# The first gate rows of two expert passes: the first expert pair's tokens gathered in other parts and banks

## The reference, cut to what matters

```python
def moe_ffn(h, expert, gate, w_gate, w_up, w_down):
    ...
    xb = h[slot_tok].reshape(n_blocks, MOE_BLOCK, D)
    def expert_block(args):
        xblk, e = args
        return (jax.nn.silu(xblk @ w_gate[e]) * (xblk @ w_up[e])) @ w_down[e]
    yb = lax.map(expert_block, (xb, block_expert))
    y = yb.reshape(n_pad, D) * slot_gate[:, None].astype(h.dtype)
    return jnp.zeros_like(h).at[slot_tok].add(y)
```

## Time and profile before

| | us |
|---|---|
| median of three runs | 1698.57 (1698.17 to 1700.7) |
| the profiled execution's own time | 1696.97 |
| its span | 1695.2 |
| TensorE busy | 1647.9 (97%) |
| ScalarE busy | 288.5 (17%) |
| VectorE busy | 448.9 (26%) |
| mean transfer rate | 352 GB/s |

### The profile page before, as it was taken

One profiled execution on the slowest core, in us unless ns is written; L12 is line 12 of the kernel. 1 busy time (PEld: TensorE's weight loads), 2 busy tenths in 40 slices (PEclk: granted clock), 3 DMA queues, 4 the chain that ended last, 5 costly groups with the idle time before them and its releaser, 6 DMA issues.

```text
span 1695.2 us, 20421 instructions
## 1 busy us (share of the span) xinstructions
PE 1647.9 (97%) x8806; PEld 940.7 (55%) x8806; DVE 448.9 (26%) x940; ACT 288.5 (17%) x584; POOL 62.4 (4%) x92
## 2 busy tenths in 40 slices
PE   9999999999899999999999999899999999999997
PEld 7784433433333785634334333348787888866554
DVE  1470000000000325300000000025266657722222
ACT  2301101101010222111011000112222122321212
POOL 4000000000000100000000000005000000000000
PEclk9999999999999999999999999999999999999999
DMA  9889999999999956899999999999254445699996
GB/s 335 327 323 376 429 428 427 426 429 427 424 430 426 390 195 241 331 426 427 429 427 427 428 425 428 427 407 331 93 199 149 153 145 198 251 403 425 424 424 282
DMA packets 88203, 597.46 MB, mean 352 GB/s; under 512 B 6072, under 2 KB 17072, under 8 KB 53920
## 3 DMA queue, kind: packets, MB, share of 16 engines
q1 hardware_dynamic: 84480, 586.30, 85.4%
q0 software_dynamic: 3616, 9.65, 1.7%
HBM read 594.88 MB, written 1.05 MB: 352 GB/s over the span
## 4 chain that ended last, share of the span: by engine, by line
PE 59%; issue 26%; DMA 12%; DVE 2%; POOL 1%; ACT 0%; SPq 0%; POOLq 0%; DVEq 0%
PE psum L952 31%; DMA ring<-in_w_gate_dram 10%; PE psum L658 8%; PE psum L645 4%; PE psum L602 3%; PE psum L935 3%; PE psum L1046 2%; DMA ring<-in_w_up_dram 1%; PE psum L652 1%; PE psum L893 1%; PE psum L1085 1%; PE psum L1062 1%; POOL rstd L3339 1%; PE psum L780 1%; PE psum L808 0%
## 5 line engine op out<-in xcount | busy, mean ns | idle before, releaser
L952 PE MATMUL psum<-ring,xT 128*64 128x512 f32 (+1 forms) x2024 | 417.2, 560 | 29.4 <-DMA ring<-in_w_up_dram 10.5
L952 PEld LDWEIGHTS psum<-ring,xT 128*64 128x64 f32 x2024 | 144.9, 137 | 273.4 <-issue 244.7
L952 PE MATMUL psum<-ring,work 128*64 128x512 f32 x992 | 219.9, 593 | 0.1
L2615 DVE TENSOR_TENSOR work<-work,psum 128x512 f32<-128x512 f32 (+1 forms) x45 | 40.9, 910 | 573.0 <-PE psum L952 567.6
L952 PEld LDWEIGHTS psum<-ring,work 128*64 128x64 f32 x992 | 70.8, 137 | 135.5 <-issue 131.6
L645 PE MATMUL psum<-xT,ring 128*128 128x256 f32 x512 | 113.6, 380 | 0.0
L1925 ACT COPY work<-psum 128x512 f32<-128x512 f32 (+1 forms) x45 | 23.2, 515 | 489.9 <-PE psum L1062 489.9
L658 PE MATMUL psum<-ring,mkv 128*128 128x256 f32 x456 | 104.9, 380 | 0.0
L645 PEld LDWEIGHTS psum<-xT,ring 128*128 128x128 f32 x512 | 96.3, 190 | 13.8 <-issue 0.8
L658 PE MATMUL psum<-ring,xT 128*128 128x256 f32 x400 | 92.0, 379 | 0.3 <-issue 0.3
L658 PEld LDWEIGHTS psum<-ring,mkv 128*128 128x128 f32 x456 | 85.7, 190 | 11.8 <-DVE work L3188 0.3
(11 more groups left out here) (378 smaller groups left out, 1646.8 us busy)
## 6 DMA issues: line engine op xcount, KB each, us to landing
ring<-in_w_down_dram SPq DMA_DIRECT2D x49, 2048.0 KB, 22.2
ring<-in_w_up_dram SPq DMA_DIRECT2D x49, 2048.0 KB, 21.8
ring<-in_w_gate_dram SPq DMA_DIRECT2D x48, 2048.0 KB, 20.3
ring<-in_w_in_dram SPq DMA_DIRECT2D x16, 2048.0 KB, 11.1
ring<-in_w_exp_up_dram SPq DMA_DIRECT2D x15, 2048.0 KB, 19.1
work<-in_w_gate_dram SPq DMA_DIRECT2D x10, 2048.0 KB, 13.1
ring<-in_w_exp_down_dram SPq DMA_DIRECT2D x10, 2048.0 KB, 20.7
work<-in_w_exp_gate_dram SPq DMA_DIRECT2D x9, 2048.0 KB, 15.6
```

Source lines behind the costliest of these rows:

```text
L952: ins = pe.matmul(to[part * CAP:(part + 1) * CAP, 0:n], lhsT=lhsT, rhs=w[:, half * n:(half + 1) * n], start=first, stop=last)
L2615: dve.tensor_tensor(by_rows(h[:, 0:F], j), in_order(silu[:, 0:F], j), in_order(u_bank[:, 0:F], j), ALU.mult).then_inc(sem("h"), 1)
```

## The change

Part 0 of the first group is gathered in two halves that are counted, copied and waited for apart: chunks 0 and 1 into `m_bank`, chunks 2 and 3 into `y_bank`. Gate chunks 0 and 1 wait for the first copy, gate chunks 2 and 3 for the second. Part 1 goes into `u_bank`: its chunks 4 and 5 are gathered behind gate chunks 0 and 1, its chunks 6 and 7 behind gate chunks 2 and 3. Gate chunks 4 to 7 wait for its copy. In passes with groups of two the semaphores `gathered` and `xe` count one more, so everything that waits on them is shifted by one (`gathers`).

```diff
-                                ... gathered=E, xe=E, ...
+                                ... gathered=E + (not pairs), xe=E + (not pairs), ...
...
+            def gathers(self, g, part):
+
+                return self.group * g + part + (self.group == 2)
...
-                def gather(g, part, to, first=0, end=None):
+                def gather(g, part, to, first=0, end=None, signals=True):
...
-                    if end is None:
+                    if signals:
                         ins.then_inc(sem("gathered"), 1)
...
-                        pe.wait_ge(sem("xe"), plus(ph.group * g + part, B["xe"]))
+                        pe.wait_ge(sem("xe"), plus(ph.gathers(g, part), B["xe"]))
                         gather(g, part, to)
...
                 elif first == 0:
-                    gather(0, 0, m_bank)
-                    gather(0, 1, y_bank, 0, 2)
+                    gather(0, 0, m_bank, 0, 2)
+                    gather(0, 0, y_bank, 2)
                     pe.wait_ge(sem("xe"), plus(1, B["xe"]))
                     up("gate", g_bank, 0, range(2))
-                    gather(0, 1, y_bank, 2)
+                    gather(0, 1, u_bank, 0, 2, False)
+                    pe.wait_ge(sem("xe"), plus(2, B["xe"]))
                     up("gate", g_bank, 0, range(2, 4))
-                    pe.wait_ge(sem("xe"), plus(2, B["xe"]))
+                    gather(0, 1, u_bank, 2)
+                    pe.wait_ge(sem("xe"), plus(3, B["xe"]))
                     up("gate", g_bank, 0, halves[1])
...
                 elif first == 0:
-                    tokens(0, 0, m_bank)
-                    tokens(0, 1, y_bank)
+                    for c, of in ((0, m_bank), (2, y_bank)):
+                        act.wait_ge(sem("gathered"), plus(c // 2 + 1, B["gathered"]))
+                        act.copy(ph.tokens(0, 0)[:, c:c + 2, :], of[:, c * P:(c + 2) * P].rearrange("p (c s) -> p c s", c=2)).then_inc(sem("xe"), 1)
+                    tokens(0, 1, u_bank)
                     gate(0)
...
-                        dve.wait_ge(sem("gathered"), plus(ph.group * g, B["gathered"]))
+                        dve.wait_ge(sem("gathered"), plus(ph.gathers(g, 0), B["gathered"]))
```

More of the change, by code:

```diff
@@ L393, in __init__ @@
                 self.per = dict(used=self.pieces, silu=E, h=E + 1, t_full=E + 1, hT=E + 1, last_part=1 + pairs, y=2 * E + 2 if pairs else E + 1, y_lo=2 * E + 2 if pairs else 0, slot_gate=E // 2 if pairs else 0,
-                                pick=TC * E // self.group, pickg=2 * E, gathered=E, xe=E, pick_turned=E // 2 if pairs else E, pickT=E // 2 if pairs else E, scattered=4, shift=1, piece=16 * self.pieces // RAW, tail=16 + self.ahead, half=2, early=32)
+                                pick=TC * E // self.group, pickg=2 * E, gathered=E + (not pairs), xe=E + (not pairs), pick_turned=E // 2 if pairs else E, pickT=E // 2 if pairs else E, scattered=4, shift=1, piece=16 * self.pieces // RAW, tail=16 + self.ahead, half=2, early=32)
                 times = MORE if more else 1
@@ L1154, in hand_out @@
                         pe.wait_ge(S("rows_in"), (32, 80)[phases.index(ph)])
-                        pe.wait_ge(sem("xe"), B["xe"] + N_EXP)
+                        pe.wait_ge(sem("xe"), B["xe"] + N_EXP + 1)
                     else:
@@ L1863, in tokens @@
                 def tokens(g, part, of):
-                    act.wait_ge(sem("gathered"), plus(ph.group * g + part + 1, B["gathered"]))
+                    act.wait_ge(sem("gathered"), plus(ph.gathers(g, part) + 1, B["gathered"]))
                     act.copy(ph.tokens(g, part), of.rearrange("p (c s) -> p c s", c=DC // ph.group)).then_inc(sem("xe"), 1)
```

## The result

The changed kernel takes 1700.86 us in the median (1699.65 to 1703.7, 20 runs), the kernel before 1698.46 us (1697.26 to 1700.7, 20 runs) on the same chip: +2.4 us, ratio 1.0016 with a 95% interval of 1.001 to 1.0022. It is slower, by a little less than the 3.4 us that I had called the bound of what can be told; with twenty runs each the difference is clear of zero. I had forecast -0.8 us. The profiled execution is 1700.63 us long, its span is the first row here; the page shows nothing else.

The account below looks back on a forecast made before the run. Weight transfers were taken to end both expert passes; an unbroken stream 0.4 us earlier in each, with TensorE's 1.16 us delay absorbed by its waits, summed to -0.8 us from 1698.57, giving 1697.8 us, range 1696.0 to 1701.2.

Parts of the forecast that it names:

- the stall: TensorE's new wait before gate chunk 4 for the copy of part 1, forecast at 0.75 us a pass.
- A2: Third early 1 MB weight transfer of a pass, issued at 137.60; forecast 1.16 us later, at 138.76.
- A0: First early 1 MB weight transfer of a pass, issued at 132.93; forecast 0.84 us earlier, at 132.09.
- A1: Second early 1 MB weight transfer of a pass, issued at 135.89; forecast 0.84 us earlier, at 135.05.
- the dry microsecond: Stretch 132.5 to 133.5 at a pass's start, transfers at only 33 GB/s; forecast to go.
- unbroken stream: Transfers running without gaps after a pass's start; forecast to begin 0.17 to 0.67 us earlier, taken as 0.4 us.
- A4: First 2 MB transfer after the four 1 MB ones, issued at 142.75; forecast issued at 143.91, flowing from 144.5.
- close, but not dry: Claim that A4, flowing from 144.5, arrives before A3 ends at 144.8, so the transfers never run empty there.
- A3: Fourth early 1 MB weight transfer of a pass, issued at 139.32; forecast issued at 140.48 and ending at 144.8.
- TensorE's delay through: Rival: TensorE's 1.16 us delay at chunk 4 reaches each pass's end, +2.3 us, 1700.9, if transfers don't end passes; chance 0.10.
- rows 3: Profile rows of TensorE's weight waits, the last just ahead of 544.99 and 1095.23, read as transfers ending each pass.
- dry twice more: Rival: A2 and A4 meet an empty queue, each losing 0.5 us; 0 to +0.6 us a pass, up to 1699.8; chance 0.18.

Follow-up runs that it names:

- e2: Changed kernel with part 1's chunks 6 and 7 gathered right behind chunks 4 and 5, ahead of gate chunks 2 and 3: 1698.62 us against 1698.53 for the kernel before.
- e3: Kernel before with only the gather of chunks 6 and 7 moved behind gate chunks 2 and 3: 1701.24 us against 1698.53.
- e5: Kernel before with four idle TensorE products ahead of expert 0's down rows in both passes: 1703.24 us against 1698.25.
- e6: Kernel before with four idle TensorE products ahead of expert 1's up rows in both passes: 1699.44 us against 1698.25.
- e7: Kernel before with four idle TensorE products ahead of expert 4's up rows in both passes: 1698.23 us against 1698.25.
- e10: Kernel before with four idle TensorE products ahead of expert 0's up rows in both passes: 1706.71 us against 1698.38.
- e4: Kernel before with four idle TensorE products ahead of gate chunk 4 in both passes: 1707.19 us against 1698.53.
- e1: Kernel before with all sixteen gather products in one run ahead of gate chunk 0: 1698.57 us against 1698.53.
- e13: Kernel before with six of the eight gather products of the first group's part 1 left out: 1697.62 us against 1698.43.

## Why the prediction was wrong

*TensorE's part was right.* Gate rows 0.90 us earlier (0.84 forecast), the stall 0.67 us (0.75), chunk 4 and A2 onward 1.09 us later (1.16); the copies, VectorE's marks and the silu moved without anyone waiting for them. A0 and A1 came 0.90 us earlier, and the dry microsecond went: 229 GB/s from 4 to 5 us behind the first gather instead of 139.

*The step that failed* is the one that follows the transfers: "From there TensorE frees 2 MB each 3.43 us and the transfers need 4.9. So the unbroken stream starts 0.17 to 0.67 us earlier". I had drawn the rate of the frees from two issues and stopped at A4. A4 (142.75) was the last issue that I weighed, as "close, but not dry", and between 146 and 160 us I had looked at no row of the transfers. The rows that I should have gone on to read, the later issues of the kernel before:

```profile
146.19 0.33 SPq L3468 DMA_DIRECT2D ring<-in_w_down_dram  x1
149.62 0.33 SPq L3468 DMA_DIRECT2D work<-in_w_up_dram  x1
155.80 0.33 SPq L3471 DMA_DIRECT2D work<-in_w_up_dram  x1
161.36 3.76 SPq L3471 DMA_DIRECT2D ring<-in_w_gate_dram  x2
```

and their sizes, with the last column the us from issue to landing (issues from 140 to 150 us):

```profile
work<-in_w_down_dram SPq DMA_DIRECT2D x1, 2048.0 KB, 9.3
ring<-in_w_down_dram SPq DMA_DIRECT2D x1, 1536.0 KB, 9.8
work<-in_w_up_dram SPq DMA_DIRECT2D x1, 1536.0 KB, 10.1
```

The gaps behind 149.62 are 6.2 and 5.6 us, since TensorE transposes and gathers the next pair there, and two of the pieces are of 1.5 MB, the rest of them having been loaded earlier. From A3's issue (139.32) up to that at 161.36 SP issues 1 + 2 + 1.5 + 1.5 + 2 = 8 MB (each 1.049 million bytes) in 22.0 us, 381 GB/s. The transfers can do 427. The second pass has one of the two smaller pieces at 2 MB, 404 GB/s by the same count: still below 427.

What the transfers moved in these 22.04 us, first in the kernel before, then in the changed one:

```profile
139.32:161.36 22.04, 22.04 (x120) 9.90 (x118) 2.16 (x5) 3.23 (x6) 0.00 (x0) 1.00 1.01 411
...
141.31:163.35 22.04, 22.04 (x120) 9.88 (x118) 2.15 (x5) 3.22 (x6) 0.00 (x0) 1.00 0.97 381
```

So in the kernel before the transfers still move more than is issued. They live on what stands in the queue at A3's issue, 0.66 MB or 1.5 us of it over the stretch. In the changed kernel they move 381, no more than TensorE's frees bring. In the second pass it is 410 against 392 GB/s by the same windows from A3's issue, and in the first pass of the other kernels it is 411 in e2, which has no stall, and 393 in e3, which has nothing but the stall. The landings of single pieces (issue plus time to landing) show where that begins. A3 lands 18.6 us behind the first gather before and 18.5 after, as I had forecast. A4, behind it, lands at 23.9 and at 24.7 (in the second pass at 24.2 and 25.5), and the five pieces that follow are 1.1 to 2.4 us late in the first pass and 1.2 to 1.3 in the second. That is the place that I had called close, but not dry. Only behind 33 us do the frees come faster than the transfers, at first a piece each 3.44 us, and a store builds up; the time to landing there rises from 8 to 10 us to 14 to 16, and e5, e6 and e7 show lateness losing its price.

*What followed from it.* The sum had +0.4 us a pass for the gain and counted TensorE's delay as taken back by its waits. The gain of A0 was spent within 3 us: e2 keeps it without the delay and is worth nothing that can be told. The delay came through: +1.17 and +1.08 us a pass, e3 shows it alone. The rival that I had named for this outcome, TensorE's delay through, had the right size (+2.3 us, 1700.9) and the right place, and I gave it 0.10. But its condition, that the transfers don't end the pass, is wrong: the last waits of rows 3 are all there. It needs only that the transfers follow TensorE at the beginning, and I had priced that case as "dry twice more" at half its size, because I looked for dry microseconds and not for the sum of what is issued. The measured 1700.86 lies inside my range of 1696.0 to 1701.2 only because the range took in this rival as its upper bound; the forecast itself had the wrong sign.

*On the rule of the Trainium skill.* The 2 us of fixed cost that the Trainium skill ("DMA: Bandwidth & Descriptors", section on the anatomy of one DMA) gives are measured there on transfers that GpSimd issues, while these are issued by SP. In e10 a 2 MB transfer that met an empty queue landed 7.3 us after its issue; less 4.9 us for its bytes at 427 GB/s that leaves 2.4 us, so the trace shows a fixed cost of nearly that size for SP's transfers too. That the estimate worked out from it, +0.3 instead of -0.8, lay on the right side was luck: it set A2's landing after the change against the end of A2's bytes before it, though the fixed cost is in both. A2 in fact landed 0.9 us earlier in the changed kernel (15.3 us behind the first gather instead of 16.2).

*Open.* Why e3, e4 and e10 lose more than their delay (1.2 us a pass for 0.74, 4.2 and 4.6 for 3.8): an empty queue may add its own cost at each restart, but no run takes that apart. Why landing times of 9 to 10 us, 2 us above that of an empty queue, are no cushion: in the kernel before, the piece ahead is still 3.5 us from landing when the one at 33.18 us is issued, and e10's issue at 31.4 us lands after 9.8 us, yet all of the lateness comes through. So it is shown that early lateness comes through, and in which stretches the bytes go missing, but how it gets through a queue that isn't empty is not shown. And whether earliness up to 25 us is paid at all, which e1, e2 and e13 leave inside their intervals.

## What to carry to other kernels

In a stage that ends bound by transfers, don't take a stall of the consumer for free before the transfers have a store of issued work. Add up the bytes that are issued, piece by piece with their sizes and gaps, from the start of the stage to the point where the time to landing begins to rise. Here they came at 381 and 404 GB/s against 427, and a stall in that stretch cost about its own length or more, however many microseconds TensorE waited for data later; behind that point the price fell to part of it and then to nothing. And when a piece of work is moved next to the wait for its own result, see what now covers that wait; here one line moved by two chunks cost what the rest of the change did not bring back.

## What the runs showed of the hardware

- A copy of 512 columns between two runs of TensorE, with nothing between, costs it 0.67 to 0.68 us: 0.03 to the copy, 0.58 for it, and the rest back.
- A run of gathering less between the gate rows (e1, the same products) brings the issues of A2 and behind it 0.35 us earlier; so the switch from gate rows to gathering and back costs TensorE about 0.35 us.
- A transfer of SP that met an empty queue landed 7.3 us after its issue with 2 MB (e10) and 4.9 us with 1 MB (e4, A2): about 2.4 us beside its bytes at 427 GB/s.
- Ahead of the first gather, with the same instructions, the span varies by 1.5 us between traces (127.55 to 129.09 us; the kernel before alone 127.62 and 128.18). What sets it was not tried; comparisons of one stage are better counted from its own first instruction.
